# One weight load held back behind a gather, and five small copies moved behind twelve transposes

## The reference, cut to what matters

```
probs = softmax(h @ w_router)
gates, idx = top_k(swapaxes(probs, 1, 2), cap)     # 64 of 512 latent, 16 of 128 context tokens per expert
xs = h[idx]
a = silu(xs @ w_gate) * (xs @ w_up)                # 1024 x 1024 each, per expert, float32
y = (a @ w_down) * gates
x = x + gate2 * zeros.at[idx].add(y)
```

## Time and profile before

| | |
|---|---|
| runs | 853.18, 854.40, 854.32 us; median 854.32 |
| profiled execution | 853.98 us, of which the trace's span is 852.1 us |
| TensorE busy | 830.2 us, 97% of the span |
| VectorE, ScalarE, GpSimd busy | 502.6, 233.3, 60.6 us |
| moved by DMA | 275.28 MB |
| experts | from about 332 us to the end |

### The profile page before, as it was taken

The page is one execution under the profiler, slowest core; times in us unless marked ns, Lnnn a source line. Parts: engine busy times, 40 slices in busy tenths (PEclk is TensorE's granted clock), DMA queues, the critical chain, the costliest instruction groups (busy, mean ns, idle before and its releaser), DMA issues.

```text
span 852.1 us, 14545 instructions
## 1 busy us (share of the span) xinstructions
PE 830.2 (97%) x6034; PEld 455.7 (53%) x6034; DVE 502.6 (59%) x1233; ACT 233.3 (27%) x462; POOL 60.6 (7%) x74
## 2 busy tenths in 40 slices
PE   6999999999999999999999999999999999999995
PEld 5798899899897876333333333333333333333322
DVE  3676552869366568876556456456456465465436
ACT  5557543544243334020110110111011011011015
POOL 1000000000000002011011011011011011010033
PEclk9999999999999999999999999999999999999998
DMA  9955625352418939999999999999999999999993
GB/s 329 303 203 190 224 82 198 113 197 75 136 34 343 367 131 326 425 409 428 415 407 430 410 410 429 411 413 423 415 411 419 419 412 417 424 409 412 427 349 147
DMA packets 51014, 275.28 MB, mean 323 GB/s; under 512 B 5210, under 2 KB 14526, under 8 KB 38788
## 3 DMA queue, kind: packets, MB, share of 16 engines
q1 hardware_dynamic: 45484, 255.68, 74.3%
q0 software_dynamic: 3936, 13.77, 5.5%
q10 hardware_dynamic: 1528, 4.90, 1.5%
HBM read 260.83 MB, written 13.57 MB: 322 GB/s over the span
## 4 chain that ended last, share of the span: by engine, by line
PE 89%; DMA 3%; DVE 3%; ACT 2%; SPq 1%; issue 1%; POOLq 0%; DVEq 0%
PE pair L2466 26%; PE pair L2069 17%; PE pair L2445 12%; PE pair L2491 12%; PE pair L2306 7%; PE pair L2500 6%; PE pair L2009 2%; PE pair L2104 2%; DMA scale_b<-in_w_mod 2%; DMA xs<-hn,gather_idx 1%; PE pair L2227 1%; PE pair L2217 1%; PE pair L2018 1%; DVE aT L1847 1%; DMA out<-x_sb 0%
## 5 line engine op out<-in xcount | busy, mean ns | idle before, releaser
L2466 PE MATMUL pair<-ring,xT 128*64 128x512 f32 x1024 | 223.9, 594 | 1.4 <-ACT xT L1126 1.4
L2466 PEld LDWEIGHTS pair<-ring,xT 128*64 128x64 f32 x1024 | 72.1, 137 | 143.9 <-issue 141.7
L2491 PE MATMUL pair<-ring,aT 128*64 128x512 f32 x512 | 113.4, 595 | 0.6 <-DVE aT L1847 0.6
L2445 PE MATMUL pair<-ring,xT 128*32 128x512 f32 x1024 | 113.4, 594 | 0.0
L1126 ACT ACTIVATE xT<-xT,mod,scale 128x64 f32<-128x64 f32 x120 | 41.4, 427 | 218.9 <-DVE xT L1847 218.9
L1847 DVE STREAM_TRANSPOSE xT<-xs 32x256 f32<-32x256 f32 x180 | 78.3, 435 | 4.4 <-DMA xs<-hn,gather_idx 1.4
L1847 DVE STREAM_TRANSPOSE aT<-act_l 32x128 f32<-32x128 f32 x256 | 77.5, 303 | 4.1
L2491 PEld LDWEIGHTS pair<-ring,aT 128*64 128x64 f32 x512 | 35.8, 137 | 76.8 <-issue 76.8
L2069 PE MATMUL pair<-hT_hi,w_hi 128*128 128x320 f32 x320 | 76.0, 319 | 0.0
L2445 PEld LDWEIGHTS pair<-ring,xT 128*32 128x32 f32 x1024 | 31.5, 110 | 79.4 <-issue 79.4
L2069 PE MATMUL pair<-hT_lo,w_hi 128*128 128x320 f32 x320 | 73.1, 310 | 0.0
(11 more groups left out here) (332 smaller groups left out, 940.6 us busy)
## 6 DMA issues: line engine op xcount, KB each, us to landing
ring<-in_w_up SPq DMA_DIRECT2D x32, 2048.0 KB, 29.0
ring<-in_w_down SPq DMA_DIRECT2D x32, 2048.0 KB, 19.7
ring<-in_w_gate SPq DMA_DIRECT2D x31, 2048.0 KB, 24.9
p1w<-in_w_mod SPq DMA_DIRECT2D x8, 2048.0 KB, 7.9
p1w<-in_w_in SPq DMA_DIRECT2D x5, 2048.0 KB, 7.9
p1w<-in_w_mod SPq DMA_DIRECT2D x7, 1024.0 KB, 11.8
x_sb<-in_x_sample SPq DMA_DIRECT2D x8, 512.0 KB, 5.8
p1w<-in_w_out SPq DMA_DIRECT2D x2, 2048.0 KB, 8.7
```

Source lines behind the costliest of these rows:

```text
L2445: ins = mm(ctx_ps[32 * g:32 * g + 32, :], xt[:, 4 * half + j, CAP_L:96], w[:, j, n * 512:(n + 1) * 512], start=half == 0 and j == 0, stop= ...
L2466: ins = mm(ps[64 * n:64 * n + 64, :], xt[:, kk, 0:CAP_L], w[:, j, n * 512:(n + 1) * 512], start=kk == 0, stop=kk == KC - 1)
L2491: ins = mm(y_ps[0][r:r + 64, :], aT[:, j, 64 * fh:64 * fh + 64], wd[:, j, n * 512:(n + 1) * 512], start=fh == 0 and j == 0, stop=fh == 1 a ...
```

## The change

SP waits, ahead of load 9 (lower half of expert 1's up matrix), until gather 1 has landed. And on DVE, in expert 0, the five copies of `choice()` stand behind `tokens(1)` and no longer ahead of it; the wait for `g2_ready` stays behind `choice()`.

```
@@ -605,6 +605,7 @@
             load_part(BY_ROWS, 3)
             sp.wait_ge(job_done, job("lg4") + 1)
             sp.wait_ge(sums_ctx, 32)
+            sp.wait_ge(xs_full[1], 16)
             load_rows(9)
             for n in range(TURNS, 6 * (E - 1)):
                 load_later(n)
@@ -1893,9 +1894,9 @@
                     ins = turned(aTc, act_c, s, 4)
                 ins.then_inc(aTc_ready, 1)
                 if k == 0:
+                    tokens(e + 1, k + 1)
                     choice()
                     dve.wait_ge(g2_ready, 2)
-                    tokens(e + 1, k + 1)
                 if k == E - 1:
                     dve.wait_ge(froot_ready, 1)
```

## The result

The changed kernel takes 858.78 us (median of 6 runs, 858.40 to 859.81), the kernel before, in the same comparison, 854.04 us (6 runs, 853.18 to 855.55). The ratio is 1.0057, with a 95% interval of 1.0046 to 1.0069: slower by some 4.9 us, or 4.7 by the medians. The profiled execution has a span of 856.8 us against 852.1.

What follows compares the result with a forecast made beforehand. The load stream was taken as the slower resource, TensorE living on a 3.7 us lead. TensorE's chain: -1.37 + 0.4 = -1.0 us; stream: 3.4 late against 3.7, -0.3 us. The later gave 854.0 us, range 852.8 to 857.0.

Steps and rivals of the forecast that it cites:

- What bounds the kernel: Experts' loop: loads come every 32.6 us, TensorE uses them every 31.5 us, and 3.7 us of lead remains at load 87.
- The hole: TensorE's idle time ahead of expert 1, waiting on gather 1: 1.37 us, claimed to close whole.
- The debt of the stream: Lateness of the weight loads from load 9 on, claimed 3.4 us, not made up, falling due at load 87 in expert 14.
- the stream is held too long: Rival, chance 0.15: gather 1 takes 6.6 us, loads from load 9 run 5.9 us late, end +2.2 us, 856.5 us.
- Gather 2: Issued at 366.4, not 360.35, after the moved copies; taking 11.2 us, it stalls expert 1's down product 0.4 us.
- The sum: Whole kernel: TensorE's own chain -1.0 us, the load stream's chain -0.3 us, giving -0.3 us overall.
- The later of the two decides: At the kernel's end, the later of TensorE's chain (-1.0 us) and the load stream's chain (-0.3 us) sets the time.
- The range: Run time of the whole kernel: 852.8 us with the full gain, to 857.0 us with both 2 us rivals covered.

## Why the prediction was wrong

- **What bounds the kernel: right.** The stream of loads is the slower resource, TensorE lives on a lead of 3.7 us. The run with two halved loads shows it from one side, the 80-row gathers from the other.
- **The hole: right in its mechanism.** It closed whole, and the chain from gather to TensorE came out as written. Its size, 1.37 us, was one execution's; the profiles show 0.4 to 1.5.
- **The debt of the stream: the first step that failed, by its size.** The step was a debt of 3.4 us: gather 4.1, load 9 alone 7.6, less 1.25 for the gather's own traffic. Measured, with the 0.83 us added: 6.7 us at load 9 (362.7 - 356.8 + 0.8) and 6.4 at load 87. The gather took 5.1 (+1.0), load 9 took 8.6 (+1.0), and of the credit only 0.3 us was left at load 87 (+0.95). Against 3.7 in hand that is 2.7 us and not a gain of 0.3: the second half of expert 14 begins at 786.40, before at 784.4, which with the 0.83 is 2.8 us late. This is the rival "the stream is held too long", with a debt above its 5.9. The price that the Trainium skill gives ("DMA: Bandwidth & Descriptors", anatomy of one DMA) made 3.2 us for the gather, an estimate from the page's figures; the 5.1 and 4.8 us measured are above it and above the value that I chose. The same page's advice (rules for kernel authors), to issue early and wait late, was borne out by the wait alone, +4.9 us.
- **Gather 2: sized well.** It landed 11.5 us after its issue (11.2 was taken) and the stall was 0.85 us (0.4).
- **The sum took the end of the program for fixed: the second step that failed, a term put at nothing.** "The later of the two decides" holds for the loop. The prediction then added nothing behind it. It had not asked what the late loads hold up after the last weight: the reads of the closing rows stand behind them on SP's queue, GpSimd's products behind those, and these now overlap VectorE's operations. That is 2.5 us in the profile, and making the products fills takes 2.9 us off. The margin was visible in the trace of before, products ending at 836.36 and the first operation with two inputs at 836.54: 0.18 us.
- **The range** ended at 857.0, since it took one cause of slowness at a time. Either failed step alone would have stayed inside it. Without the collision the loss is 2.0 us, which is 856.0 beside the 854.04 of the kernel before, and the collision's 2.5 us alone would make 856.5.
- **Open:** why 80-row gathers slow the stream, some 1.7 us of what the move costs by itself, and why only 0.3 of the 1.25 us of the gather's traffic was left as credit. The profiled pair adds up to 3.0 us in the loop and 2.5 behind it, 5.5 in all, less the 0.83 by which this execution ran ahead; the ratio's interval is 3.9 to 5.9 us, so each part is known to some tenths only.

## What to carry to other kernels

When transfers and TensorE are both at 100%, compare landings with needs early and late in the run: the difference is a stock, and each microsecond in which the queue of loads stands empty is drawn from it and falls due hundreds of microseconds later. A wait put on the queue's engine to speed up one small transfer empties the queue for that transfer, its completion and the start of the next load. And follow the delay past the loop: what is queued behind the last load shifts too, and may run into work that it had just missed. A hole that a change is to close should be read from several executions: here it was 1.37 us in the one profile and 0.4 to 1.5 in all.

## What the runs showed of the hardware

- A gather of 512 KB took 4.8 to 5.1 us with the rest of one load and a quarter of another queued ahead of it, 8.2 us beside one 2 MB load, and 10.6 to 11.9 us beside a full queue of them.
- A 2 MB load issued to a nearly empty queue took 8.0 to 9.3 us, where it takes 5.0 us of a full stream.
- Indirect gathers of 80 rows and not 128 brought the traffic from 417 to 399 GB/s with the DMA engines as busy, and 13 of them cost 11.1 us.
- A VectorE operation with two inputs of 128 x 3 elements in SBUF took 0.16 us, and up to 2.31 us while GpSimd multiplied two tiles from SBUF; beside GpSimd's fills it took 0.16 us. Three in a row took 1.04, 2.29 and 2.28 us: each can be held anew.
- TensorE's granted clock was 0.58 for 2.1 us behind a wait of 2.14 us, and 1.00 behind waits of 1.69 and, in another expert, 3.12 us.
